# Second operand area at a multiple of 512 bytes behind the first; first modulation blocks summed along rows by VectorE

## The reference, cut to what matters

```
def rmsnorm(x, g):
    y = x * lax.rsqrt(jnp.mean(x * x, axis=-1, keepdims=True) + EPS)
    return y * g

def modulate(x, g, shift, scale):
    return rmsnorm(x, g) * (1.0 + scale[:, None, :]) + shift[:, None, :]

def adaln(c, w_mod, b_mod):
    mod = jax.nn.silu(c) @ w_mod + b_mod        # (1, 1024) @ (1024, 6144)
    return jnp.split(mod, 6, axis=-1)

sh_m, sc_m, g_m, sh_f, sc_f, g_f = adaln(c, mod_w, mod_b)
h = modulate(x, norm_mix, sh_m, sc_m)
... _split(h @ w_in, IN0_SIZES) ...
```

## Time and profile before

| | us |
|---|---|
| median of 3 runs | 2409.58 (2409.21 to 2412.39) |
| the profiled execution | 2409.51 |
| its span, first to last instruction | 2407.8 |
| TensorE busy in the span | 2346.8 (97%) |
| VectorE (DVE) | 1344.7 (56%) |
| ScalarE (ACT) | 936.5 (39%) |
| GpSimd (POOL) | 1120.5 (47%) |

### The profile page before, as it was taken

How to read it: one execution, slowest core, us unless ns; L and a number is a source line. 1 busy time by engine, 2 the same in 40 slices (tenths; PEclk the granted TensorE clock), 3 DMA queues, 4 the chain that set the end, 5 groups by cost and what they waited for, 6 DMA issues and landing times.

```text
span 2407.8 us, 33483 instructions
## 1 busy us (share of the span) xinstructions
PE 2346.8 (97%) x11717; PEld 1909.7 (79%) x11717; DVE 1344.7 (56%) x2132; ACT 936.5 (39%) x1495; POOL 1120.5 (47%) x528
## 2 busy tenths in 40 slices
PE   7999999999999999999999899999999999999998
PEld 6777788888776778888888678888888968888886
DVE  6786777772457651111158857263567473736455
ACT  3467332222336733222244544222256383322222
POOL 2346354554536435444446534444454473444443
PEclk9999999999999999999999999999999999999999
DMA  7530446763321023223232122323232202232322
GB/s 292 204 123 2 158 170 208 251 209 114 113 71 62 27 71 106 97 95 99 94 103 88 53 105 91 103 89 103 88 120 93 92 19 79 87 105 87 105 87 79
DMA packets 69951, 261.48 MB, mean 109 GB/s; under 512 B 7888, under 2 KB 8400, under 8 KB 68816
## 3 DMA queue, kind: packets, MB, share of 16 engines
q1 hardware_dynamic: 66672, 250.48, 30.9%
q10 hardware_dynamic: 3168, 9.50, 1.1%
HBM read 257.86 MB, written 2.10 MB: 108 GB/s over the span
## 4 chain that ended last, share of the span: by engine, by line
PE 88%; DVE 5%; issue 2%; POOL 1%; DMA 1%; ACT 1%; POOLq 1%; DVEq 0%; SPq 0%; ACTq 0%
PE bank L740 26%; PE bank L742 26%; PE bank L741 26%; PE bank L912 2%; PE bank L931 2%; PE bank L900 2%; POOL w_lo L663 1%; DMA first_mods<-in_first 1%; POOLq L728 1%; DVE acc L1717 1%; DVE bank L2340 1%; PE bank L842 0%; POOL prob L681 0%; DVE bank L1983 0%; DVE prob L1896 0%
## 5 line engine op out<-in xcount | busy, mean ns | idle before, releaser
L663 POOL TENSOR_TENSOR w_lo<-raw,w_hi 128x1024 fp32r<-128x1024 f32 x377 | 941.7, 2506 | 1176.2 <-ACT w_hi L1293 1174.7
L740 PE MATMUL bank<-h_hi,w_hi 128*128 128x512 f32 x1768 | 699.0, 395 | 13.6 <-DVE h_lo L1764 7.8
L742 PE MATMUL bank<-h_hi,w_lo 128*128 128x512 f32 x1768 | 693.1, 392 | 0.0
L741 PE MATMUL bank<-h_lo,w_hi 128*128 128x512 f32 x1768 | 693.0, 392 | 0.0
L1293 ACT ACTIVATE w_hi<-raw 128x1024 fp32r<-128x1024 f32 x377 | 391.8, 1051 | 420.8 <-PE bank L742 378.5
L740 PE MATMUL bank<-g_hi,w_hi 128*128 128x512 f32 x1072 | 421.1, 393 | 0.0
L742 PE MATMUL bank<-g_hi,w_lo 128*128 128x512 f32 x1072 | 420.9, 393 | 0.0
L741 PE MATMUL bank<-g_lo,w_hi 128*128 128x512 f32 x1072 | 417.3, 389 | 0.0
L740 PEld LDWEIGHTS bank<-h_hi,w_hi 128*128 128x128 f32 x1768 | 335.0, 189 | 94.0 <-DVE h_lo L1764 8.6
L742 PEld LDWEIGHTS bank<-h_hi,w_lo 128*128 128x128 f32 x1768 | 334.9, 189 | 71.0
L741 PEld LDWEIGHTS bank<-h_lo,w_hi 128*128 128x128 f32 x1768 | 335.4, 190 | 69.2 <-issue 0.5
(11 more groups left out here) (302 smaller groups left out, 2417.9 us busy)
## 6 DMA issues: line engine op xcount, KB each, us to landing
raw<-in_panels SPq DMA_DIRECT2D x377, 512.0 KB, 3.4
modraw<-in_blocks SPq DMA_DIRECT2D x80, 512.0 KB, 4.0
first_mods<-in_first SPq DMA_DIRECT2D x4, 2048.0 KB, 22.1
x<-in_x SPq DMA_DIRECT2D x1, 2048.0 KB, 7.9
w<-in_w ACTq DMA_DIRECT2D x1, 2048.0 KB, 9.0
out<-yout ACTq DMA_DIRECT2D x8, 256.0 KB, 2.2
mask<-in_causal ACTq DMA_DIRECT2D x1, 1024.0 KB, 7.1
mask<-in_dilated ACTq DMA_DIRECT2D x1, 1024.0 KB, 6.9
```

Of the source, the lines that this page charges most:

```text
L663: pool.tensor_tensor(w_lo[:, slot, :], raw[:, slot, :], w_hi[:, slot, :].bitcast(F32), ALU.subtract)\
L740: pe.matmul(out, w_h, m_h, start=start, stop=False)
L741: pe.matmul(out, w_h, m_l, start=False, stop=False)
L742: return pe.matmul(out, w_l, m_h, start=False, stop=stop)
```

## The change

Five things. (1) The start of the second operand area is rounded up to a multiple of 512 bytes behind the first; with a new 64-byte tensor, modhalf, it moves from 113,728 to 114,176 bytes. (2) TensorE spreads csil over the rows of two PSUM banks, CROW (spread_crow). (3) The blocks of the first batches are stored with outputs on the rows, and VectorE sums each along its row, in two halves with an accumulator (sum_rows); block 0 of batches 2 and 3 stays with TensorE (first_block). (4) first_mod adds the two half sums and the bias, one column at a time, with the second half sum and the bias as per-row scalars. (5) x * rstd is formed for blocks 0 and 1 by VectorE and for 2 to 7 by POOL from a copy of rstd, rb0; ScalarE makes both h_hi and an unrounded copy in PSUM (FIRST_H; the last two are VectorE's), and VectorE subtracts. A root table load is put ahead of the weight splits; lruw and the later loads of ScalarE wait for the last h_lo; crow is no longer loaded but copied from CROW.

```diff
         bank = [ctx.enter_context(nc.psum_tensor(f"bank{n}", [P, 512], F32)) for n in range(8)]
-        FIRST_BANK = [bank[7], bank[4], bank[3], bank[7]]
-        CHAIN = bank[6]
+        FIRST_COLUMN, FIRST_H = bank[4], (bank[3], bank[5])
+        CROW = (bank[6], bank[7])
         x = sb("x", [P, KB, T])
...
         modacc = sb("modacc", [P, 2])
+        modhalf = sb("modhalf", [P, 2, 4])
         cols = sb("cols", [P, N_COLS])
...
         small = sb("small", [P, QB, 24])
+        place[0] += -(place[0] - hx) % 512
         gx = place[0]
...
         sq0 = s("sq0", [P, KB, T], 0)
-        modsum = s("modsum", [P, 4, P], 16)
+        rb0 = s("rb0", [P, T], 16)
         sq = s("sq", [P, 2, T], 0)
...
                 pool.tensor_tensor(sq0[:, 2 * n, :], sq0[:, 2 * n, :], sq0[:, 2 * n + 1, :], ALU.add).then_inc(two_added, 1)
-            split_from(0, P_OUT0 + 2)
+            split_from(0, 3)
+            pool.wait_ge(rb0_ready, 1)
+            for k in range(2, KB):
+                pool.tensor_tensor(sq0[:, k, :], x[:, k, :], rb0[:, :], ALU.mult).then_inc(xr_pool_ready, 1)
+            split_from(3, P_OUT0 - 1)
             weights(0, 0)
...
                 return pe.matmul(out, w_l, m_h, start=False, stop=stop)
-            def first_batch(n):
+            def first_block(n):
                 pe.wait_ge(first_landed[n], 16)
-                if n == 3:
-                    pe.wait_ge(first_added, 1)
+                if n > 2:
+                    pe.wait_ge(mods_ready, n)
                 for k in range(KB):
-                    pe.matmul(FIRST_BANK[n][:, 0:1], first_mods[n][:, 0, P * k:P * k + P], csil[:, k:k + 1],
-                              start=(k == 0), stop=(k == KB - 1))
-                pe.wait_ge(mod_summed, n + 1)
-                for w in range(1, 4):
-                    m = pe.matmul(FIRST_BANK[n][:, w:w + 1], modsum[:, w, :], ones[:, 0:1], start=True, stop=True)
+                    m = pe.matmul(FIRST_COLUMN[:, n:n + 1], first_mods[n][:, 0, P * k:P * k + P], csil[:, k:k + 1],
+                                  start=(k == 0), stop=(k == KB - 1))
                 m.then_inc(mod_used, 1)
+            def spread_crow():
+                for k in range(KB):
+                    m = pe.matmul(CROW[k // 4][:, P * (k % 4):P * (k % 4) + P], csil[:, k:k + 1].broadcast_to((P, P)),
+                                  ident[:, :], start=True, stop=True)
+                m.then_inc(crow_spread, 1)
             def by_k(p, m_hi, m_lo, ready, ks):
...
             pe.wait_ge(csil_ready, 1)
+            spread_crow()
             pe.wait_ge(filled, 1)
...
             m.then_inc(sums_ready, 1)
-            first_batch(0)
             spread(0, bank[5], QB)
-            first_batch(1)
-            by_k(0, h_hi, h_lo, 0, (0, 1, 2, 3))
-            first_batch(2)
-            first_batch(3)
+            by_k(0, h_hi, h_lo, 0, (0, 1))
+            first_block(2)
+            by_k(0, h_hi, h_lo, 0, (2, 3))
+            first_block(3)
             by_k(0, h_hi, h_lo, 0, (4, 5, 6, 7))
...
                 for k in range(KB):
-                    if r == 0 and k == 4:
+                    act.wait_ge(t_ready, KB * (H_OF[r] - 1) + k + 1)
+                    act.activation(h_hi[:, k, :], tn[:, k % 2, :], ACT.Identity, bias=shift(r, k)).then_inc(h_hi_ready, 1)
+            def first_high():
+                for k in range(KB):
+                    if k == 4:
                         split_hi(3)
-                    act.wait_ge(t_ready, KB * H_OF[r] + k + 1)
-                    act.activation(h_hi[:, k, :], tn[:, k % 2, :], ACT.Identity, bias=shift(r, k)).then_inc(h_hi_ready, 1)
+                    act.wait_ge(mods_ready, k // 2 + 1)
+                    if k < 2:
+                        act.wait_ge(xr_ready, k + 1)
+                    else:
+                        act.wait_ge(xr_pool_ready, k - 1)
+                    act.activation(h_hi[:, k, :], sq0[:, k, :], ACT.Identity, bias=shift(0, k), scale=gain(0, k))\
+                        .then_inc(h_hi_ready, 1)
+                    if k >= KB - 2:
+                        continue
+                    if k == 1:
+                        act.wait_ge(rb0_ready, 1)
+                    elif k >= 2:
+                        act.wait_ge(h_lo_ready, k - 1)
+                    act.activation(FIRST_H[k % 2][:, :], sq0[:, k, :], ACT.Identity, bias=shift(0, k), scale=gain(0, k))\
+                        .then_inc(h32_ready, 1)
             def project(p0, r):
...
                 act.activation(sq0[:, n, :], x[:, n, :], ACT.Square).then_inc(squares_ready, 1)
+            act.activation(root[:, 6 * QB - 1:6 * QB], one, ACT.Sqrt)
             for p in range(3):
                 split_hi(p)
...
             m.then_inc(root_ready, 1)
+            first_high()
+            act.wait_ge(h_lo_ready, KB)
             act.dma_start(lruw[:, :, :, :], A["lruw"]).then_inc(lru_landed, 16)
-            h_high(0)
-            act.dma_start(crow[:, :], A["crow"]).then_inc(crow_landed, 16)
             act.dma_start(peT[:, :, :], A["pe"]).then_inc(pe_landed, 16)
             act.dma_start(w2[:, :, :], A["w2"]).then_inc(w1_landed, 16)
-            act.wait_ge(mod_used, BATCHES)
             act.dma_start(w1[:, :, :, :], A["w1"]).then_inc(w1_landed, 16)
...
                 elif p == 3:
-                    act.wait_ge(crow_landed, 16)
-                    act.activation(crow[:, :], crow[:, :], ACT.Silu).then_inc(crow_ready, 1)
+                    for half in range(2):
+                        m = act.activation(crow[:, T * half:T * half + T], CROW[half][:, :], ACT.Copy)
+                    m.then_inc(crow_ready, 1)
                 elif p == 4:
...
                 dve.drain()
-            def weighted(blocks_, n, to, used, between=None):
-                w = blocks_.rearrange("p n (k m) -> p n k m", m=P)
-                part = CHAIN[:, 0:n * P].rearrange("p (n m) -> p n m", m=P)
-                dve.tensor_scalar(part, w[:, :, 0, :], csil[:, 0:1], None, MUL)
-                for k in range(1, KB):
-                    if k == KB // 2 and between is not None:
-                        between()
-                    dve.drain()
-                    if k == KB - 1 and used is not None:
-                        dve.wait_ge(mod_used, used)
-                    m = dve.scalar_tensor_tensor(out=part if k < KB - 1 else to, in0=w[:, :, k, :], scalar=csil[:, k:k + 1],
-                                                 in1=part, op0=MUL, op1=ADD)
-                m.then_inc(mod_summed, 1)
-                dve.drain()
-            def sum_first(n, between=None):
+            def sum_rows(n, ws):
                 dve.wait_ge(first_landed[n], 16)
-                weighted(first_mods[n][:, 1:4, :], 3, modsum[:, 1:4, :], n if n else None, between)
+                for w in ws:
+                    for half in range(2):
+                        row = first_mods[n][:, w, T * half:T * half + T]
+                        m = dve.scalar_tensor_tensor(out=row, in0=row, scalar=1.0, in1=CROW[half][:, :],
+                                                     op0=MUL, op1=MUL, accum_out=modhalf[:, half, w:w + 1])
+                if ws[-1] == 3:
+                    m.then_inc(mod_summed, 1)
             def sum_pair(m, landed):
...
                 return v_.rearrange("p (w k) -> p w k", w=2)[:, :, 2 * n:2 * n + 2]
-            def first_h(n):
-                dve.wait_ge(mod_used, n + 1)
-                dve.tensor_tensor(by_part(modv[:, 0:2 * KB], n), FIRST_BANK[n][:, 0:4].rearrange("p (w k) -> p w k", w=2),
-                                  by_part(cols[:, COLS["modb"]:COLS["modb"] + 2 * KB], n), ADD).then_inc(first_added, 1)
-                dve.drain()
-                at = COLS["g0mix"] + 2 * n
-                dve.scalar_tensor_tensor(out=gains[:, 2 * n:2 * n + 2], in0=modv[:, KB + 2 * n:KB + 2 * n + 2], scalar=1.0,
-                                         in1=cols[:, at:at + 2], op0=ADD, op1=MUL)
-                if n == 0:
-                    dve.wait_ge(rstd_ready, 1)
+            def first_mod(n):
+                dve.drain()
+                biased, own = COLS["modb"], COLS["g0mix"]
+                for w, at in enumerate((2 * n, 2 * n + 1, KB + 2 * n, KB + 2 * n + 1)):
+                    to, bias = modv[:, at:at + 1], cols[:, biased + at:biased + at + 1]
+                    if n >= 2 and w == 0:
+                        dve.wait_ge(mod_used, n - 1)
+                        dve.tensor_scalar(to, FIRST_COLUMN[:, n:n + 1], bias, None, ADD)
+                    else:
+                        dve.tensor_scalar(to, modhalf[:, 0, w:w + 1], modhalf[:, 1, w:w + 1], bias, ADD, ADD)
                 dve.drain()
                 for k in (2 * n, 2 * n + 1):
-                    dve.scalar_tensor_tensor(out=tn[:, k % 2, :], in0=x[:, k, :], scalar=gain(0, k), in1=bank[5][:, :],
-                                             op0=MUL, op1=MUL).then_inc(t_ready, 1)
-                dve.drain()
```

(60 more changed lines are left out.)

## The result

The changed kernel takes 2397.39 us (median of 4 runs, 2396.64 to 2397.70), the kernel before 2410.89 beside it (2409.21 to 2412.39): ratio 0.9944 [0.9932, 0.9957]. The forecast was 2402.0, the range 2399.0 to 2407.5. The profiled execution took 2397.53 us, span 2395.8 us (12.0 us under the span before), and its chain has 85% on TensorE, near the 88% of the earlier trace rows.

What follows compares the result with a forecast made beforehand. TensorE's panel products bound the kernel, so only its waits in the first 50 us pay: hidden(0) 8.1 us earlier, less 0.6 given back, takes 7.5 off 2409.51, giving 2402.0 us; range 2399.0 to 2407.5.

Steps and rivals of the forecast that it cites:

- The new row: TensorE's eight spreading products into banks 6 and 7, ahead of the square sums: cost 0, up to 4.1 us without that cover.
- Half-row sums: VectorE's 128x512 sums at the start: 0.67 us each from start to start, ends 0.61 and 0.75; 28 halves in all.
- the 0.6 given back in the forecast: Taken off the 8.1 us gain for small waits of VectorE on later work, leaving 7.5 us.
- first_mod: VectorE's six one-column operations per turn: 0.8 us, not held by POOL; 2.3 us a turn if held.
- What is late next: w1, issued after the eighth h_lo, lands at 57.3 us; hidden(0) waits 1.2 us and starts 8.1 us earlier.
- Rival 3: TensorE's start: gaps between block pairs keep the clock low, all 72 products at 0.43 us; +4 us, 2413.5; chance 0.08.
- Rival 2: VectorE keeps its lag in later work: gain only 3.3 to 5.7 us, time 2404 to 2406; chance 0.13.
- The step that failed: Rounding the second operand area's address: no effect on TensorE's g products, 0, bounds about 1 us either way.

Runs made afterwards that it cites:

- wide_first_mod: Changed kernel with first_mod's six single-column operations written as three on several columns, plus one copy for TensorE's column: 2399.66 us, 0.9957 of the kernel before.
- all_early: Changed kernel with peT, w2, w_small and cmask issued while ScalarE waits for the third batch's gains, w1 right behind its last h_hi: 2395.57 us.

## Why the prediction was right about the start and wrong about the time

- **The new row:** right. It ends at 8.3 us, ahead of the square sums, and costs nothing.
- **Half-row sums:** at 0.61, the fast end of 0.61 to 0.75; 28 x 0.06 = 1.7 us gained. (Half of 1.14 is 0.57; 0.61 is half of the 1.22 that the row lasts. The times given for the two ends leave out the 0.6 given back in the forecast, and 1.7 off 46.9 is 45.2, not 45.6.)
- **first_mod:** unheld, as argued, but mis-sized: a turn takes 1.2 to 1.5 us in place of 0.8, the last one too (1.2, with POOL idle). The row behind the 0.8 had small operations 0.23 us apart, which is 1.4 for six. Turn 0 lies beside the spread and costs nothing; the other three lose 0.4 us each and eat most of what the sums gained: last h_lo 46.6 for 46.9. That the two nearly cancel is luck (and 43.9 + 2 x 0.67 + 2 x 0.7 is 46.6, not 46.9). The Trainium skill (Advanced Engine Details and Errata, "2x-2p Requirements") excludes a dimension of one; the trace agrees, with 0.20 to 0.27 us for a single column beside POOL and the same in the last turn without it. The four columns of wide_first_mod were added by another operation and do not test this.
- **What is late next:** right. w1 was issued at 47.95 and landed 8.7 us later; 0.87 us of waiting for 1.2.
- **Rival 3, the clock:** not here. After the gap before 34.27 the products go on at 0.34 and 0.23 us at once. The Trainium skill (TensorE: Matmul & The Clock Gate, "HAM oscillation") tells of a kernel whose every piece starts cold after a long wait for its data; this trace shows one slow stretch, the first nine products. Three other runs with this start had a second one: some eight products at 0.43 us, from 35.4 us on in all_early, 37.9 in wide_first_mod and 41.8 with all moved by 64, whose trace has these:

```profile
42.19 0.63 PE L753 MATMUL bank<-h_hi,w_lo 128*128 128x512 f32 x1
42.62 0.63 PE L751 MATMUL bank<-h_hi,w_hi 128*128 128x512 f32 x1
```

So such a fall can come with this start, but nowhere did it last for 72 products, as in rival 3.
- **Rival 2, VectorE stays behind:** no. Of the 8.66 us, 8.3 are left in the stretch 153 to 161 (same instruction, both traces). Then 1.6 us go in the attention of layer 0, between 172 and 180, where the unrounded kernel, which has the same start, loses nothing against the kernel before (8.56 at 172 and 8.57 at 180). The windows of the two, the changed one first, differ in the granted clock, on average between its two levels in the first and at the upper one in the second (third column from the right; TensorE's busy time stands behind the length), after a nearly equal pause:

```profile
170.00:175.00 5.00, 2.85 (x14) 1.39 (x14) 4.30 (x20) 4.47 (x15) 4.08 (x4) 0.81 0.00 0
175.00:180.00 5.00, 5.00 (x48) 3.70 (x46) 1.86 (x6) 2.34 (x6) 2.04 (x2) 0.85 0.00 2
```

```profile
170.00:175.00 5.00, 3.08 (x30) 2.17 (x32) 4.11 (x19) 4.53 (x14) 4.08 (x5) 1.00 0.00 0
175.00:180.00 5.00, 5.00 (x44) 3.38 (x44) 3.01 (x11) 3.66 (x10) 3.16 (x3) 1.00 0.02 5
```

- **The step that failed:** "In 20 us of dense work g_hi and h_hi products are busy the same 18.14 us, 64 bytes apart or not: 0. Bounds: a thousandth of the products' pace either way, about 1 us". The runs put 7.6 - 2.6 = 5.0 us in its place, five times the bound. The reading failed twice. A product is counted 0.39 us while the next starts 0.23 us after it, so in a window of dense products the busy time is nearly the same whatever the pace. The count beside it is too coarse for a pace 1% apart: g_hi has 59 in the window shown, but 60 from 630 to 650 us in the same trace. And the page had a hint without any window: the two rows of g_hi at 393 ns stand 3.8 and 3.6 us of busy time above that of g_lo at 389, from the same area. That alone does not name the address (h's first product is slower than its others too, 395 ns against 392), but it was no ground for a bound of 1 us. I also asked only what the line changes against the kernel before (64 to 0), not where the area would lie without it (128): that is the larger part of its worth.

So the sum by terms: 8.66 at hidden(0), 5.0 for the rounding, and 1.7 of loss left over between them and 12.0, where 0.6 was given back. The 1.6 us between 172 and 180 are nearly as much by themselves; the other gains and losses nearly cancel and were not taken apart. Of the 13.5 us by medians the remaining 1.5 are spread between executions. Of the 6.0 us by which the forecast was off, the rounding is 5.0.

## What to carry to other kernels

A pace is read from the starts of consecutive instructions, or from a group's mean duration, never from busy time in a window of overlapping ones. A line that moves an address is a change to every instruction that reads there: multiply one nanosecond by the number of products before costing it at nothing, and ask where the buffer would lie without it. Small VectorE operations beside POOL can be held for a microsecond or two in one form and not in another: here single columns by tensor_scalar were free, four columns by tensor_tensor were not.

## What the hardware showed that I had not expected

- The pace of TensorE's dense products (128x512) depends on the distance between the moving tile and the weight tiles: 227 ns from start to start at 0 and 256 bytes over a multiple of 512, 230 in two of three places at 64, 233 in all at 32, 128 and 192. Token panels (weights from the area, 256 wide) go from 120 ns at 0, 128 (the mean of its three places) and 256 to 118 at 32 and 192 and 113 at 64. All these are worked out from consecutive starts in the traces. No offset tried is fast for both, and why the distance matters is open.
- The window 20 to 32 us of the changed kernel shows a granted clock of 1.00, though nine products in it stand 0.43 us apart, as in the earlier trace rows, and the next 0.23: the trace's record of the clock begins at 29.7 us, so that column does not show the slow start.
- Executions of one kernel differ by 1 to 6 us. The two kernels of the windows above, whose work is the same there, differ in that stretch by the clock granted after a nearly equal pause.
